# Prologue sums on TensorE, shift products on GpSimd and ScalarE, and idle PSUM pairs at four stage starts of a two-block transformer kernel

## The reference

```
m = silu(c) @ w + b                                  # shift, scale (and gate) of each modulated norm
h = rmsnorm(x, g) * (1 + scale) + shift              # rmsnorm: x * rsqrt(mean(x*x) + 1e-6) * g
proj = h @ w_in; b_gate, c_gate, u, z = split(proj)  # first layer, 4096 columns
y = b_gate * causal_dwconv(c_gate * u) * silu(z)
x = x + gate * (y @ w_out)
...
x = rmsnorm(x, final_norm_g)
h = rmsnorm_2(x, g_mix); z = h @ w_in_2              # 512 pooled columns, then q, k, v
y_pool = pool_mixer(u_pool, w_grp, scale)            # window means of 2, 4, 8, 16, four 128x128 matmuls
gates = sigmoid(h @ w_gate + b_gate)
x = x + (gates_a * (y_pool @ w_bp) + gates_b * (y_attn @ w_ba)) @ w_out_2
x = x + square(relu(rmsnorm_2(x, g_ffn) @ w_up)) @ w_down
```

## Time and profile before

| what | value |
|---|---|
| median of 3 runs | 2939.66 us (2937.34 to 2942.59) |
| profiled execution | 2939.87 us, span 2938.1 us |
| PE | 2786.5 us busy, 95% |
| DVE | 1303.8 us, 44% |
| ACT | 1059.0 us, 36% |
| POOL | 728.9 us, 25% |
| DMA | 228.39 MB, mean 78 GB/s |

### The profile page before, as it was taken

One profiled execution on the slowest core, in us unless ns is written; L12 is line 12 of the kernel. 1 busy time (PEld: TensorE's weight loads), 2 busy tenths in 40 slices (PEclk: granted clock), 3 DMA queues, 4 the chain that ended last, 5 costly groups with the idle time before them and its releaser, 6 DMA issues.

```text
span 2938.1 us, 37071 instructions
## 1 busy us (share of the span) xinstructions
PE 2786.5 (95%) x13484; PEld 2217.6 (75%) x13484; DVE 1303.8 (44%) x1610; ACT 1059.0 (36%) x1429; POOL 728.9 (25%) x355
## 2 busy tenths in 40 slices
PE   4999998999999998899989999999999999999999
PEld 2888886887777776677867777777877888888887
DVE  7544543105777775551015554544433415143241
ACT  4222222224545553332136767665223212121121
POOL 0222222122545553122221211111222222222122
PEclk8999999999999999999999999999999999999999
DMA  5333321333111122112320101002521111111112
GB/s 211 129 121 129 107 93 43 127 131 136 51 63 60 49 79 100 36 60 98 121 84 34 37 29 36 29 29 94 190 75 43 50 43 50 50 47 46 50 50 100
DMA packets 62707, 228.39 MB, mean 78 GB/s; under 512 B 6960, under 2 KB 7600, under 8 KB 62128
## 3 DMA queue, kind: packets, MB, share of 16 engines
q1 hardware_dynamic: 62640, 227.49, 21.8%
HBM read 187.62 MB, written 39.85 MB: 77 GB/s over the span
## 4 chain that ended last, share of the span: by engine, by line
PE 51%; issue 39%; POOL 5%; ACT 3%; DVE 2%; DMA 0%; POOLq 0%; ACTq 0%; DVEq 0%; SPq 0%
PE PS L617 35%; POOL WL L1953 5%; PE PS L817 5%; PE PS L789 2%; PE PS L766 2%; PE PS L751 2%; PE PS L722 1%; PE PS L954 1%; PE PS L935 1%; DVE bC L1699 1%; PE PS L898 1%; ACT bN L1220 0%; PE PS L771 0%; PE PS L913 0%; ACT WH L1082 0%
## 5 line engine op out<-in xcount | busy, mean ns | idle before, releaser
L1953 POOL TENSOR_TENSOR WL<-WR,WH 128x1024 fp32r<-128x1024 f32 x215 | 527.0, 2451 | 1997.6 <-ACT WH L1082 1875.4
L617 PE MATMUL PS<-HH,WH 128*128 128x512 f32 x2256 | 715.4, 399 | 54.8 <-issue 25.5
L617 PE MATMUL PS<-HL,WH 128*128 128x512 f32 x2256 | 701.3, 392 | 0.0
L617 PE MATMUL PS<-HH,WL 128*128 128x512 f32 x2256 | 700.2, 392 | 0.0
L617 PEld LDWEIGHTS PS<-HH,WH 128*128 128x128 f32 x2256 | 420.3, 190 | 158.1 <-issue 53.7
L617 PEld LDWEIGHTS PS<-HL,WH 128*128 128x128 f32 x2256 | 427.6, 190 | 90.8
L617 PEld LDWEIGHTS PS<-HH,WL 128*128 128x128 f32 x2256 | 426.9, 189 | 90.8
L1082 ACT ACTIVATE WH<-WR 128x1024 fp32r<-128x1024 f32 x214 | 226.3, 1057 | 623.0 <-PE PS L617 461.5
L1699 DVE TENSOR_TENSOR_SCAN bC<-bN,EPSC 128x256 f32<-128x256 f32 (+7 forms) x128 | 233.7, 1833 | 60.5 <-ACT bN L1220 56.8
L617 PE MATMUL PS<-GH,WH 128*128 128x512 f32 x752 | 231.7, 389 | 3.1 <-DVE TMP L1902 3.1
L1971 POOL TENSOR_TENSOR bB<-bB,bC 128x256 f32<-128x256 f32 (+7 forms) x128 | 180.4, 1417 | 207.9 <-DVE bC L1699 207.9
(11 more groups left out here) (232 smaller groups left out, 3127.5 us busy)
## 6 DMA issues: line engine op xcount, KB each, us to landing
WR<-wst SPq DMA_DIRECT2D x215, 512.0 KB, 3.3
TMP<-mods SPq DMA_DIRECT2D x48, 512.0 KB, 3.4
MRAW<-mods SPq DMA_DIRECT2D x16, 512.0 KB, 11.2
X<-xt SPq DMA_DIRECT2D x4, 1024.0 KB, 9.0
x_b<-X SPq DMA_DIRECT2D x8, 512.0 KB, 4.7
v_t<-VS SPq DMA_DIRECT2D x8, 512.0 KB, 5.4
k_hi<-KSH SPq DMA_DIRECT2D x8, 512.0 KB, 4.9
k_lo<-KSL SPq DMA_DIRECT2D x8, 512.0 KB, 5.7
```

Of the source, the lines that this page charges most:

```text
L617: last = pe.matmul(PS[:, dst0 + q:dst0 + q + HALF], l, rr[:, k * S + q:k * S + q + HALF], start=a, stop=z)
L1953: pool.tensor_tensor(WL[slot][:, :], WR0[:, :], WH[slot][:, :].bitcast(F32), ALU.subtract).then_inc(w_lo, 1)
```

## The change

It has these parts:

1. **Sums.** PE adds the squares itself: eight pairs of matmuls with ones accumulate the tiles of XSQ in PSUM pair 2 as ACT delivers them; DVE's seven adds go.
2. **Shift and scale.** DVE computes only the scale's dot product for tiles 1 to 7 (both for tile 0), with the scale's bias added for all tiles in advance and folded into one coefficient instruction, and no longer two tiles ahead. POOL multiplies the shift rows 1 to 7 with silu(c); ACT sums each product by its accumulator and adds the bias.
3. **Second chunk.** It is loaded into a buffer of its own, WR1 (the place of HH's last tile), early in the DMA stream, and cast and split before the fill. ACT's identities move behind the fill.
4. **Pooled chunks.** ACT casts the next weights ahead of the pooled tile of the group before.
5. **Idle pairs.** The group matmuls use pairs 2, 3, 1, 2, and only the second chunk behind them waits for their outputs. The first q, k, v chunks use pairs 0, 1, 0, with the group sums inside them in pairs 2 and 3. The first w_out chunk uses pair 2.
6. **FFN start.** One chunk after the other in place of `two_chunks`, the norm's sum behind the fifth step of the first.
7. The residual loops of DVE are written out, since the pair is no longer a function of the loop's parity.

```diff
+GP_AT = (2, 3, (C_GP + 1) % 2, 2)
...
+POOL_MODS = range(1, KT)
+DVE_MODS_A = N_MODS_A - len(POOL_MODS)
...
-         ("qkv2", 24 + GA_LATE, 0, 0), ("ab", 4, 4, 0), ("wo", 4, 4, 0), ("ff", 32, 32, 0))
+         ("qkv2", 23 + GA_LATE, 1, 0), ("ab", 4, 4, 0), ("wo", 3 + C_WO % 2, 4 - C_WO % 2, 1), ("ff", 32, 32, 0))
...
+def out_pair(name, base, c):
+    if name == "wo":
+        return (2, 0) if c == 0 else ((base + c) % 2, (c - 1) // 2)
+    return (base + c) % 2, c // 2
...
+        WR1 = nc.alloc_sbuf_tensor_at("WR1", [P, D], F32, offset=HL_AT - 4 * S)
...
             for k in range(KT):
-                if k == 3:
-                    load_w(1)
+                if k == 1:
+                    sp.dma_start(WR1[:, :], wst[1]).then_inc(ld_w1, 16)
                 for m in (k, KT + k):
                     sp.dma_start(MRAW[:, m * D:(m + 1) * D], mods[m]).then_inc(ld_ma[k], 16)
...
-            sum_squares(KT - 1, T[2])
+            for k in range(KT):
+                pe.wait_ge(sq, max(k, 1))
+                for h in (HALF, 0) if k == KT - 1 else (0, HALF):
+                    last = pe.matmul(PS[:, 2 * S + h:2 * S + h + HALF], ONES[:, :], kt(XSQ, k)[:, h:h + HALF],
+                                     start=k == 0, stop=k == KT - 1)
...
                 pe.wait_ge(p_ml, g + 1)
-                if g < 2:
-                    pe.wait_ge(free[g], u[g])
-                else:
-                    pe.wait_ge(p_yl, g - 1)
-                last = mm3((g % 2) * S, WH[cg % 2][:, b], WL[cg % 2][:, b], MXH, MXL, g, True, True)
+                if g == 2:
+                    pe.wait_ge(free[GP_AT[2]], u[GP_AT[2]])
+                elif g == 3:
+                    pe.wait_ge(p_yl, 1)
+                last = mm3(GP_AT[g] * S, WH[cg % 2][:, b], WL[cg % 2][:, b], MXH, MXL, g, True, True)
...
-            pe.wait_ge(p_yl, 4)
             with pe.Fori(0, KT) as n:
                 chunk(2 * n + C_GP, s0, s0, n + u[s0])
+                pe.wait_ge(p_yl, 4)
                 chunk(2 * n + (C_GP + 1), s1, s1, n + u[s1], YPH, YPL, nk=4)
...
-            for n in range(3):
-                chunk(C_QKV2 + n, (C_QKV2 + n) % 2, 0, ud[0] + n)
-                if n == 0:
-                    pe.wait_ge(d_st, 16)
-                if n < 2:
-                    group_sums(n + 1)
+            for n, (pair, used) in enumerate(((0, ud[0]), (1, ud[1]), (0, ud[0] + 1))):
+                pe.wait_ge(free[pair], used)
+                for k in range(KT):
+                    step(C_QKV2 + n, (C_QKV2 + n) % 2, pair, HH, HL, k)
+                    if k == 3 and n == 1:
+                        pe.wait_ge(d_st, 16)
+                        pe.wait_ge(free[2], ud[2])
+                        group_sums(1, 2 * S)
+                    if k == 3 and n == 2:
+                        group_sums(2, 3 * S)
...
-            chunks("wo", C_WO, KT, GH, GL, operand=(g_lo, KT))
+            u, s0, s1 = USED["wo"], C_WO % 2, (C_WO + 1) % 2
+            chunk(C_WO, s0, 2, u[2], GH, GL, operand=(g_lo, KT))
+            chunk(C_WO + 1, s1, s1, u[s1], GH, GL)
...
-                        two_chunks(C_FF, slots, slots, [u[p] for p in slots], (f_lo, FILL["ffn"]),
-                                   early=lambda: sum_squares(SQ["wo"] + KT, T[1]))
+                        pe.wait_ge(free[slots[0]], u[slots[0]])
+                        for k in range(KT):
+                            pe.wait_ge(f_lo, FILL["ffn"] + k + 1)
+                            step(C_FF, slots[0], slots[0], HH, HL, k)
+                            if k == 4:
+                                sum_squares(SQ["wo"] + KT, T[1])
+                        chunk(C_FF + 1, slots[1], slots[1], u[slots[1]])
...
+            act.wait_ge(ld_w1, 16)
+            act.activation(WH[1][:, :], WR1[:, :], ACT.Identity).then_inc(w_hi, 1)
...
+            def shift_sum(k):
+                if k in POOL_MODS:
+                    act.wait_ge(mod_prod, k - POOL_MODS[0] + 1)
+                    row_k = MRAW[:, k * D:(k + 1) * D]
+                    links(act.activation(row_k, row_k, ACT.Identity, accum_out=col(MOD, k)))
+                    links(act.activation(col(MOD, k), col(MOD, k), ACT.Identity, bias=vec("mod_b", k)))
+                if k == KT - 1:
+                    act.wait_ge(w_lo, 2)
+            fill_hi("a", 0, before=shift_sum)
...
+                if g:
+                    pooled_hi(g - 1)
                 act.activation(TP, PAIR[c % 2], ACT.Identity).then_inc(free[c % 2], 1)
-                act.wait_ge(p_mx, g + 2)
-                act.activation(kt(MXH, g), T[3], ACT.Identity).then_inc(p_mh, 1)
...
-            for k in range(1, KT):
-                dve.wait_ge(sq, k)
-                if k > 1:
-                    dve.wait_ge(sq_added, k - 1)
-                dve.tensor_tensor(T[2], T[2], kt(XSQ, k), ALU.add).then_inc(sq_added, 1)
...
-                for m in (k, KT + k):
-                    modulation(MOD[:, m:m + 1], MRAW[:, m * D:(m + 1) * D])
+                for m in (KT + k,) if k in POOL_MODS else (KT + k, k):
+                    modulation(col(MOD, k) if m == k else col(COEF, k), MRAW[:, m * D:(m + 1) * D])
...
-            fill_lo("a", 1, lambda k: col(COEF, k), 0, before=two_ahead)
+            fill_lo("a", 1, lambda k: col(COEF, k), 0, before=shift_and_scale)
...
+            for k in POOL_MODS:
+                pool.wait_ge(ld_ma[k], 32)
+                row_k = MRAW[:, k * D:(k + 1) * D]
+                pool.tensor_tensor(row_k, row_k, CB, ALU.mult).then_inc(mod_prod, 1)
```

145 lines of the change are left out of this document (84 added, 61 removed).

## The result

The changed kernel takes 2916.97 us, median of 4 runs (2916.26 to 2918.36); the kernel before, run beside it, 2939.3 us. The ratio is 0.9928 with a 95% interval of 0.9914 to 0.9941: faster, by 22 us (0.7%). Forecast were 2919.7 us with a range of 2907 to 2927. The profiled execution has a span of 2915.2 us, 22.9 less than before.

What follows compares the result with a forecast made beforehand. TensorE, busy 95% of the span, was taken as the bound, leaving idle time and slow-clock matmuls to win. Terms 2.2 - 0.2 - 5.9 - 6.0 - 3.1 - 7.2 = -20.2 from 2939.87 gave 2919.7 us, range 2907 to 2927.

Steps and rivals of the forecast that it cites:

- The sums end at 27.0: Prologue: TensorE adding eight tiles of squares itself ends at 27.0, about where the sums ended before (27.32).
- They free VectorE: Prologue: the sums on TensorE gain nothing by themselves but take seven adds off VectorE.
- 1.1 + 5 x 2.34 = 12.8 us, all added to VectorE: Prologue: GpSimd products left after the root block VectorE for their whole length, 12.8 us; third chunk +2.2 us.
- They hide behind VectorE: Prologue: ScalarE's row sum, bias and high part take 2.8 us a tile, under VectorE's 3.85.
- The rival in which they set the pace: Prologue: ScalarE's sums exceed 3.85 us a tile, prologue 7 us later, total 2927; chance 0.20 shared with late weights.
- The rival without any cost of turns: Prologue: GpSimd's turns cost VectorE nothing, prologue -10.5 us, total 2907; chance 0.14.
- The rival of the low clock: Prologue and further chunks: TensorE stays at 1.2 GHz, third chunk at 93.3, with two further chunks 2955 us; chance 0.02.
- Pooling and groups: Pooled chunks -0.2 us (0 to -4); group matmuls in idle pairs -5.9 us (-4.5 to -6.3).
- The scores start 8.2 earlier: First q, k, v chunks: scores start at 1525.9 instead of 1534.05; the place's term is -6.0 us.
- ScalarE sits until 1531.4, where I estimate it was wanted at 1529: q, k, v stage: a late weight load holds ScalarE, leaving -6.0 us (-5 to -8.2) for the place.
- a gap of 2 us ahead of the first scores: q, k, v stage: sign of a right forecast, a TensorE gap of 2 us standing before the first scores.
- w_out and FFN: First w_out chunk in idle pair 2: -3.1 us; first FFN chunks one after the other: -7.2 us.

Runs made afterwards that it cites:

- the run of the FFN start: The changed kernel with its first two FFN chunks interleaved again and the norm's sums inside them: 2925.49 us, ratio 0.9956.
- the last two experiments: Changed kernel plus PSUM root, three tiles ahead, early cast, earlier keys' sums: 2897.80 us; the same with the first stage's third-chunk cast ahead of the eviction: 2901.0 us.
- the run on the coefficient's form: The changed kernel with the one-column coefficient made from one tile input and two scalars instead of two tile inputs: 2917.73 us, ratio 0.9926.

## Why the prediction was right, and where its sizes were off

The forecast, 2919.7 us, lies 2.7 us above the result. Its mechanism for each place was the one that the traces show; four terms were met within 0.3 us, three were off.

- **Sums.** "The sums end at 27.0": they end at 26.4, and at 24.9 to 26.4 in the experiments that keep them. "They free VectorE": true, but only the run with the adds back shows how. They are worth 2.4 us, by way of GpSimd.
- **Turns.** The step "1.1 + 5 x 2.34 = 12.8 us, all added to VectorE" is the term that was mis-sized. Measured are 9.5 us. The rows show why: after the root five instructions are stretched, 30.02 by 1.40, 32.62 by 2.15, 36.04 by 1.95, 38.24 by 2.05 and 41.49 by 2.08, 9.6 us together. A turn added some 2.1 us and not the 2.34 of a whole product, and fewer products were left behind the root, with GpSimd's first split at 18.10 and not at 19.6. That is 3.3 us less, and the first scaled tile at 30.0 instead of 30.6 makes 0.6; without turns the stretch from there to the third chunk is 37.3 us, where the prediction had 36.0, which takes 1.3 back. 2.2 - 3.3 - 0.6 + 1.3 = -0.4; measured -0.2. The root's time hardly counts by itself: an earlier root only leaves more products behind it, and in the run of the FFN start a root 1.0 us earlier moved nothing.
- **ScalarE's sums.** "They hide behind VectorE": yes. One sum takes 1.04 and 0.19 us and the bias 0.30, and leaving out the products while ScalarE still sums moved the third chunk to 66.01. The rival in which they set the pace is out.
- **The rival without any cost of turns** forecast a third chunk at 66.6 and 2907 us. Leaving the products out made its condition true and gave 66.01 and 2904.9 us. Its condition did not hold in the changed kernel; its price was right to 0.6 us by two errors that nearly cancel, a first tile 1.9 us earlier than assumed (28.7 against 30.6) and a stretch behind it 1.3 longer.
- **The rival of the low clock** did not come: TensorE's pairs of matmuls last 1.05 us from 44.95 until 52.4 and 0.62 from 53.2 on, with a granted clock of 0.50 from 50 to 52 and 1.00 from 54 on.
- **Pooling and groups.** Forecast -6.1 together, measured -6.5. The fourth pooled chunk waits for the pair, as the step said, and the wait ahead of the last group (3.30, forecast 3.4) brings one slow stretch instead of two (granted clock 0.67 from 1345 to 1350; before, 0.80 from 1350 to 1355 and 0.66 from 1355 to 1360). No run undoes these two edits singly, so their terms rest on the landmarks of the two traces.
- **q, k, v.** "The scores start 8.2 earlier": 8.35. "ScalarE sits until 1531.4, where I estimate it was wanted at 1529": the wait was longer than that estimate, 3.42 us on ScalarE and 3.88 on TensorE, and 4.3 of the 8.35 were given back instead of 2.2. Two runs took it away by an earlier cast: TensorE's 3.88 fell to under 0.5 and to 0.56, so the late load is its cause. The sign "a gap of 2 us ahead of the first scores" came out (1.76); that this is VectorE's low part and that the split can meet it was not foreseen.
- **w_out and FFN.** Forecast -3.1 and -7.2, measured -3.3 and -7.2; the second is confirmed by undoing it, the first is read from the traces alone.
- **Between prologue and pooling** nothing was forecast and -1.6 us appeared, in two steps behind waits at 506 and at 693. In the latter TensorE's first matmul pair behind the wait takes 1.19 us before and 0.73 now, on unchanged code, with a granted clock of 0.76 from 693 to 700 before and 1.00 from 692 to 700 now. The same place differed between kernels of one code by 2.8 us (the last two experiments). So it is the granted clock; what sets it, and whether the change has any part in it, is open.

The sum of the forecast was right by 2.7 us, and a part of that is chance: a prologue that was forecast 2.4 too dear and a clock that gave 1.6 stand against a weight that came later than estimated (2.0).

## What to carry to other kernels

Before moving VectorE work to GpSimd, ask which of both engines' instructions read two SBUF tiles. While they do, the move is a trade of GpSimd's whole time against VectorE's, here 9.5 us of waiting for seven times 1.35 = 9.5 of work; put one of VectorE's inputs in an idle PSUM bank, and the same move pays (here 6 us, 70.35 against 76.38). Letting VectorE work ahead while it waits for the root as well made it 10 us here, a part of which might be had with the dot products left on VectorE. When a gap at a stage start is closed, look at the next weight: its load, cast and split have to start a chunk earlier as well, and where GpSimd's split falls matters as much as when it is issued. And an edit worth less than some 3 us is to be judged by its place in the trace, since the clock behind later waits moves the total by as much.

## What the runs showed of the hardware that was not expected

- GpSimd and VectorE pass the turn after every instruction. In the changed kernel seven products take 20.09 us, 2.87 each for 2.34 of work, and VectorE gets in once between each two, if only with one column.
- Keeping one operand in PSUM costs VectorE nothing: 1.22 and 1.28 us for 128x1024 from SBUF and from PSUM alike.
- Not every form with one SBUF input is exempt. With one column, the instruction with two scalars took 0.27 us beside a product (33.76 in the run on the coefficient's form). With eight columns, where 0.16 us is its undisturbed length, it waited for the end of the split at 19.44, in the run with the adds back:

```profile
20.32 2.32 DVE L1633 TENSOR_SCALAR MOD<-VEC 128x8 f32<-128x8 f32 x1
```

  and with 256 columns beside the split at 1524.68 of the changed kernel:

```profile
1525.74 1.44 DVE L1918 TENSOR_SCALAR dP<-dP,SM 128x256 f32<-128x256 f32 x1
```

  where 128x384 takes 0.42 undisturbed. The Trainium skill, in the section named above, has this too: the scalar form can enter a mode that uses both port pairs, when its operands meet certain conditions. The two waits agree with that; whether a single column misses the conditions, no run here shows.
- At the very start the granted clock reads 1.00 from the first matmul, but only three of the sums' matmul records fall into the window from 10 to 12 us and six into that from 16 to 18, with TensorE shown busy throughout. Which of the two columns to believe there, no run tells. Windows of the changed kernel (busy, PEclk, DMA share, GB/s):

```profile
10.00:12.00 2.00, 2.00 (x3) 1.00 1.02 426
...
16.00:18.00 2.00, 2.00 (x6) 1.00 1.02 408
```
